# Router logits from the added rows, tile by tile, with two loads re-placed, in a two-layer diffusion block on one core

## The reference

```python
def modulate(h, shift, scale):
    return h * (1 + scale) + shift

def expert_choice_moe(h, w_router, w_gate, w_up, w_down):
    cap = EC_CAPACITY * T // N_EXPERTS
    aff = jax.nn.softmax((h @ w_router).astype(jnp.float32), axis=-1)
    top_w, top_idx = lax.top_k(aff.transpose(0, 2, 1), cap)
    xg = jax.vmap(lambda hb, ib: hb[ib])(h, top_idx)
    ...

# in hybrid_layer
y_l = gated_merge(...)                       # branches -> sum -> @ w_out
x = x + mod_l[2] * y_l
x = x + mod_l[5] * expert_choice_moe(modulate(rms_norm(x, norm2), mod_l[3], mod_l[4]),
                                     moe_router, moe_w_gate, moe_w_up, moe_w_down)
```

## Time and profile before

| | us |
|---|---|
| median of 3 runs | 2647.32 |
| lowest and highest run | 2635.97, 2648.03 |
| profiled execution, its own time | 2637.7 |
| its span in the trace | 2635.9 |
| PE busy | 2479.0 (94%) |
| DVE busy | 1055.8 (40%) |
| ACT busy | 680.8 (26%) |

### The profile page before, as it was taken

One profiled execution on the slowest core, in us unless ns is written; L12 is line 12 of the kernel. 1 busy time (PEld: TensorE's weight loads), 2 busy tenths in 40 slices (PEclk: granted clock), 3 DMA queues, 4 the chain that ended last, 5 costly groups with the idle time before them and its releaser, 6 DMA issues. The chain is left out here.

```text
span 2635.9 us, 41045 instructions
## 1 busy us (share of the span) xinstructions
PE 2479.0 (94%) x17556; PEld 1564.9 (59%) x17556; DVE 1055.8 (40%) x2307; ACT 680.8 (26%) x1348; POOL 87.6 (3%) x145
## 2 busy tenths in 40 slices
PE   5999999999899899999999999999999999999998
PEld 3888877778686444443444588876677643333432
DVE  4545354344774313223231564445348431111113
ACT  3621232222633111111111362143236311010101
POOL 1000100000000000000100000100000000000000
PEclk9999999999999999999999999999999999999999
DMA  6111456151553999897989312322216379999996
GB/s 217 57 49 33 141 197 202 61 168 47 195 175 115 392 346 386 309 396 296 383 331 367 116 41 65 72 94 73 72 57 206 134 288 410 409 409 409 409 409 276
DMA packets 241827, 580.72 MB, mean 220 GB/s; under 512 B 11462, under 2 KB 120240, under 8 KB 240624
## 3 DMA queue, kind: packets, MB, share of 16 engines
q1 hardware_dynamic: 232160, 550.21, 56.0%
q0 software_dynamic: 9488, 27.90, 3.3%
HBM read 554.94 MB, written 23.13 MB: 219 GB/s over the span
## 5 line engine op out<-in xcount | busy, mean ns | idle before, releaser
L1040 PE MATMUL ps<-h_hi,m_lo 128*128 128x512 f32 (+1 forms) x1152 | 347.4, 373 | 2.0 <-DVE arena L2261 1.7
L1481 PE MATMUL ps<-arena 128*32 128x512 f32 x1740 | 259.2, 593 | 1.6 <-ACT arena L1923 1.1
L1482 PE MATMUL ps<-arena 128*32 128x512 f32 x588 | 258.0, 593 | 0.0
L1040 PEld LDWEIGHTS ps<-h_hi,m_lo 128*128 128x128 f32 x1152 | 208.6, 190 | 52.3 <-issue 13.7
L1013 PE MATMUL ps<-m_lo,h_hi 128*128 128x256 f32 (+1 forms) x1248 | 233.7, 289 | 5.2 <-DVE m_lo L2234 2.9
L1040 PE MATMUL ps<-h_lo,m_lo 128*128 128x512 f32 (+1 forms) x576 | 205.5, 357 | 0.0
L1013 PEld LDWEIGHTS ps<-m_lo,h_hi 128*128 128x128 f32 x1248 | 196.6, 195 | 13.7 <-issue 9.7
L1627 PE MATMUL ps<-arena 128*64 128x512 f32 x832 | 187.8, 597 | 11.1 <-DMA arena<-in_moe_w_up 8.5
L1013 PE MATMUL ps<-m_lo,h_lo 128*128 128x256 f32 (+1 forms) x624 | 177.5, 284 | 0.0
L1481 PEld LDWEIGHTS ps<-arena 128*32 128x32 f32 x1740 | 70.3, 110 | 164.2 <-issue 160.7
L1013 PE MATMUL ps<-h_hi,m_lo 128*128 128x512 f32 (+1 forms) x512 | 141.9, 354 | 7.8 <-DVE h_lo L2339 6.9
(11 more groups left out here) (407 smaller groups left out, 4498.8 us busy)
## 6 DMA issues: line engine op xcount, KB each, us to landing
arena<-in_moe_w_up SPq DMA_DIRECT2D x101, 1024.0 KB, 13.0
arena<-in_moe_w_gate SPq DMA_DIRECT2D x100, 1024.0 KB, 11.8
arena<-in_moe_w_down SPq DMA_DIRECT2D x100, 1024.0 KB, 12.8
ring<-in_w_in SPq DMA_DIRECT2D x42, 1024.0 KB, 5.3
arena<-in_ada_w SPq DMA_DIRECT2D x37, 1024.0 KB, 5.6
oT<-in_moe_w_up SPq DMA_DIRECT2D x27, 1024.0 KB, 14.9
oT<-in_moe_w_down SPq DMA_DIRECT2D x24, 1024.0 KB, 9.0
oT<-in_moe_w_gate SPq DMA_DIRECT2D x16, 1024.0 KB, 8.4
```

Source lines behind the costliest of these rows:

```text
L1040: last = mm(to, w[:, k, cols], h[:, k, seg], start=n == 0 and k == 0, stop=n == 2 and k == KD - 1)
L1481: mm(ps[r][32 * b:32 * b + 32, :], c_xg[:, k, j, 32 * b:32 * b + 32], w, start=k == 0, stop=k == KD - 1)
L1482: last = mm(ps[r][96:128, :], c_xg[:, k, j, 32 * r:32 * r + 32], up[:, kk, 512:1024], start=k == 0, stop=k == KD - 1)
```

## The change

1. The router logits are made from the added rows themselves. With r the reciprocal root of a row, g the gain and s the shift, (r x g + s) W = r (x (g W)) + s W. DVE makes `r_gain` = g W and `r_sum`, a partial sum of s W, at the end of `merge` (`router_scaled`, each layer); PE sums the latter over partitions with one product of ones inside the output products, and DVE keeps it (`router_bias`). Per tile PE transposes `x_sb` (8 transposes into two banks), ACT copies one bank and DVE the other, PE makes 8 products with the 128x128 block as stationary operand and 16 moving columns, and DVE applies r and the bias (`logits_kept`). The logits come out with tokens on partitions, so the copy out, the turn back and the four-group sum are gone. Tiles 0 and 1 of the order don't wait for the root.
2. `kept_running(ps[5], 6)` stands behind the logits in both layers. The five fillers ahead of layer 1's transposes are gone.
3. Three late pieces move to the latent attention (7 becomes 10), and all other ten stand behind the transposes of the affinities.
4. The sixth expert load of layer 0 and all behind it wait for `rows_in`, the landing of the first three row fetches. The ninth no longer waits for `lg_up`.
5. Small: `work` is set to -1 behind the softmax's subtraction, two clears of PSUM banks go away, the others clear 260 columns.

```diff
-        ADA = {"first": 8, "na": 20, "mla": 7, "route": 13}
-        UNITS_AHEAD = 2
+        ADA = {"first": 8, "na": 20, "mla": 10, "route": 10}
+        UNITS_AHEAD, LOADS_AHEAD = 2, 5
...
             def route_loads():
-                for h in ada_late("route")[:3]:
-                    late_load(h)
                 sp.wait_ge(y_up, 2 * NQ[0])
-                for h in ada_late("route")[3:10]:
+                for h in ada_late("route")[:7]:
                     late_load(h)
                 sp.wait_ge(y_ok, 2 * NQ[0])
-                late_load(ada_late("route")[10])
-                for h in ada_late("route")[11:]:
+                late_load(ada_late("route")[7])
+                for h in ada_late("route")[8:]:
                     sp.wait_ge(ada_up, h - 7)
                     late_load(h)
...
                     if l == 0 and n == PAIR_SLOTS:
                         sp.wait_ge(xn2_out, 16 * NT)
-                        sp.wait_ge(lg_up, 1)
...
+                    if l == 0 and n == LOADS_AHEAD:
+                        sp.wait_ge(rows_in, 48)
...
+            def router_logits(l):
+                n, y0 = NQ[l], before("y_ok", l)
+                def bank_read(bank):
+                    return y0 + max(q for q in range(2 * n) if 2 + q % 4 == bank) + 1
+                def turned(ti):
+                    t = q_tiles(l)[ti]
+                    first, second = ((ps[6], ps[7]), (ps[1], ps[2]))[ti % 2]
+                    pe.wait_ge(y_ok, max(y0 + n + ti + 1, bank_read(2) if ti % 2 else 0))
+                    if ti >= 2:
+                        pe.wait_ge(h_lat, before("h_lat", l) + ti - 1)
+                        pe.wait_ge(h_ctx, before("h_ctx", l) + ti - 1)
+                    for bank, up, ks in ((first, hl_up, range(4)), (second, hc_up, range(4, KD))):
+                        for k in ks:
+                            last = tr(bank[:, tile(k % 4)], x_sb[:, t, tile(k)], ident)
+                        last.then_inc(up, 1)
+                def logits(ti):
+                    pe.wait_ge(h_lat, before("h_lat", l) + ti + 1)
+                    pe.wait_ge(h_ctx, before("h_ctx", l) + ti + 1)
...
+                    for k in range(KD):
+                        last = mm(ps[(0, 3)[ti % 2]][:, 0:E], xT[ti % 2][:, k, :], r_gain[:, s, k, :], start=k == 0, stop=k == KD - 1)
+                    last.then_inc(lg_up, 1)
+                turned(0)
+                turned(1)
+                for ti in range(n):
+                    logits(ti)
+                    if ti + 2 < n:
+                        turned(ti + 2)
+                kept_running(ps[5], 6)
...
             def route(l):
-                if l == 0:
-                    late_product(ada_late("route")[3])
...
                 last.then_inc(affT_up, 1)
                 if l == 0:
-                    for h in ada_late("route")[5:]:
-                        late_product(h)
-                        late_turned(h - 1)
-                    late_turned(ada_late("route")[-1])
+                    late_products(ada_late("route"))
                     kept_running(ps[5], 3)
...
+            def normed_and_routed(l):
+                s, n = 2 * l + 1, NQ[l]
+                turned_copied(l, 0)
+                scaled(s, n - 2)
+                turned_copied(l, 1)
+                mean(s, n - 1)
+                logits_kept(l, 0)
+                turned_copied(l, 2)
+                scaled(s, n - 1)
+                for ti in range(1, n):
+                    logits_kept(l, ti)
+                    if ti + 2 < n:
+                        turned_copied(l, ti + 2)
...
                 v.tensor_tensor(aff[:, q0:NT, :], lg, st[:, 48 + q0:48 + NT].unsqueeze(2).to_broadcast([P, nt, E]), ALU.subtract
                                 ).then_inc(aff_sh, 1)
+                if NSEG[l] > 1:
+                    link(v.memset(work[0:48, :], -1.0))
```

More of the change, by code:

```diff
@@ L374, in ada_zeroed @@
         def ada_zeroed(h):
-            return 1 + sum(h >= ada_first(stage) for stage in list(ADA)[1:])
+            return 1 + sum(h >= ada_first(stage) for stage in list(ADA)[1:3])
         def late_sums(h):
@@ L1077, in kept_running @@
                     mm(bank[:, :], ident, cst[:, 0:512], start=True, stop=True)
-            def norm_transposes(l):
-                s = 2 * l + 1
-                if l == 0:
[L1083 to L1093, removed]
-                        for k in ks:
[L1095 to L1102, removed]
-                        pe.wait_ge(h_lat, before("h_lat", l) + k - 1)
-                    for t in range(CT, NT):
-                        last = tr(ps[2 + k % 2][:, tile(t - CT)], xn2[:, t, tile(k)], ident)
-                    last.then_inc(hl_up, 1)
-                    if CTX_NORMS[s]:
-                        if k >= 2:
-                            pe.wait_ge(h_ctx, before("h_ctx", l) + k - 1)
-                        for t in range(CT):
-                            last = tr(ps[4 + k % 2][:, tile(t)], xn2[:, t, tile(k)], ident)
-                        last.then_inc(hc_up, 1)
-                    if k == 5:
-                        logits(range(4))
-                logits(range(4, KD)).then_inc(lg_up, 1)
@@ L1401, in merge @@
                         for n, k in enumerate(range(KD) if half else OUT_K):
+                            if (q, n) == (1, 4):
+                                pe.wait_ge(lgT_ok, before("lgT_ok", l) + 1)
+                                mm(ps[6][:, 0:NSEG[l] * E], ones, r_sum[:, 0:NSEG[l], :].rearrange("p a b -> p (a b)"), start=True, stop=True
+                                   ).then_inc(lg_up, 1)
                             for row in gate_rows_beside(l, q, n):
@@ L1811, in scattered_rows_squared, with turned_copied @@
                 rooted(s, NORMS[s] - 1)
-            def modulate(l):
-                s = 2 * l + 1
-                for k in range(KD):
-                    act.wait_ge(hl_up, KD * s + k + 1)
-                    do(hT[:, k, LAT], ps[2 + k % 2][:, :], ACT.Identity, scale=scl[:, 1, k, 0:1],
-                       bias=modT[l][:, 24 + k, 0:1]).then_inc(h_lat, 1)
+            def turned_copied(l, ti):
+                if ti >= 2:
+                    act.wait_ge(lg_up, before("lg_up", l) + ti)
+                act.wait_ge(hl_up, before("hl_up", l) + KD + ti + 1)
+                do(xT[ti % 2][:, 0:4, :].rearrange("p a b -> p (a b)"), ps[(6, 1)[ti % 2]][:, :], ACT.Copy).then_inc(h_lat, 1)
             def modulated_high(l):
@@ L2307, in cleared @@
                 for bank in banks:
[L2308 removed]
+                    last = v.memset(bank[:, 0:260], 0.0)
                 last.then_inc(ada_zero, 1)
@@ L2320, in gains, with router_scaled @@
                                               ALU.add, ALU.mult)
-            def modulate(l):
-                s = 2 * l + 1
-                if CTX_NORMS[s]:
-                    for k in range(KD):
-                        dve.wait_ge(hc_up, KD * sum(CTX_NORMS[:s]) + k + 1)
-                        if k == 0:
-                            v.memset(work[0:48, :], -1.0)
-                        v.tensor_scalar(hT[:, k, CX], ps[4 + k % 2][:, 0:CTX], scl[:, 1, k, 1:2], modT[l][:, 24 + k, 1:2],
-                                        ALU.mult, ALU.add).then_inc(h_ctx, 1)
+            def router_scaled(l):
+                dve.wait_ge(small_in, before("small_in", l) + 48)
+                for s in range(NSEG[l]):
+                    v.tensor_tensor(r_gain[:, s, :, :], router[:, 0:KD, :], scl[:, 1, :, s].unsqueeze(2).to_broadcast([P, KD, E]), ALU.mult)
+                    last = v.tensor_tensor(r_shift[:, s, :, :], router[:, 0:KD, :], modT[l][:, 24:32, s].unsqueeze(2).to_broadcast([P, KD, E]), ALU.mult)
+                link(last)
+                for s in range(NSEG[l]):
+                    last = v.tensor_reduce(r_sum[:, s, :], r_shift[:, s, :, :].rearrange("p k e -> p e k"), AX_X, ALU.add)
+                last.then_inc(lgT_ok, 1)
```

94 lines of the change are left out of this document (43 added, 51 removed).

## The result

The changed kernel took 2659.9 us (median of 6 runs, 2657.8 to 2665.1), the kernel before 2642.2 beside it (2636.0 to 2648.2): ratio 1.0068, 95% interval 1.0046 to 1.0090. It is slower, by 12 to 24 us. The forecast was 2644 within 2633 to 2656, with 0.88 for no change: wrong. The kernel before has three of its runs at 2636 to 2637 and three at 2647 to 2648, and its profile is one of the lower; the changed kernel's runs lie in one place. The changed kernel's profiled execution took 2658.8, its span 2657.0 against 2635.9, so 21.1 us have to be found.

A forecast was written before the change was run, and what follows sets the result against it. PE, busy 94% of the span, was taken to bound the kernel, with loads in layer 1's experts; +3.8 + 0.5 - 2.2 - 0.8 - 0.7 = +0.6 us on 2637.7 gave 2638.3, stated as 2644 for two run places, range 2633 to 2656.

The forecast's parts named there:

- The logits, layer 0: Layer 0's router logits: 14.8 us on PE at 0.116 us a record, then six fillers of 5.3; +0.5 us net.
- Layer 1: Layer 1's routing: logits 9.2 us, then six fillers to 2110.0; affinities' transposes 0.7 us earlier, the experts shifting likewise.
- TensorE's clock falls in the logits: Rival, both layers' logits: 1.2 GHz over their second half and three fillers each, +17 us, 2655; chance 0.06.
- The pieces and the bias: Three late pieces paid in layer 0's latent attention, +3.8 us; bias product in the output products, 0.23 us per layer.
- The fillers eat the gain: Behind layer 0's logits: softmax ready by 854.2, but six fillers delay the affinities' transposes to 856.8, against 856.29 before.
- The fetches: Layer 0's row fetches with five loads ahead: rows at 890.6 against 892.87, -2.2 us, between -3.8 and +2.1.
- The gather behind it: Layer 0's transposes of fetched rows, 6.28 us before: faster after a shorter PE wait, -0.8 us, between 0 and -2.
- Fewer loads ahead: Start of layer 0's experts: loaded weights stay more than one pair ahead, so PE shouldn't wait: 0 us.
- The runs in two places: Whole-kernel times lie at 2636 to 2638 or 2647 to 2648; the new median could fall on either, so 2644.
- The range: Whole-kernel time: 2633 (overlap at the lower place) to 2656 (the clock's case in part, or +8 at the upper place).
- the overlap: Rival, both layers' logits: small products overlap at 0.066 us a record, -7.4 us in all, 2631 to 2637; chance 0.08.

The follow-up runs named there:

- e1: The changed kernel with each logits product reading its router columns eight times over (128 moving columns instead of 16); 2641.8 us, ratio 0.9985.
- e9: The kernel before, with layer 1's five fillers ahead of the transposes replaced by twenty products of 16 columns; 2650.8 us, ratio 1.0019.
- e8: The kernel before with only the load holding added: five expert loads ahead of the rows' first fetch, the others behind; 2635.3 us, ratio 0.9988.
- e4: The changed kernel with layer 0's expert loads no longer held back behind the row fetches; 2665.3 us, ratio 1.0080.
- e3: The changed kernel with 128 moving columns in the logits products and two fillers instead of six; 2634.9 us, ratio 0.9964.
- e2: The changed kernel without the six fillers behind the logits; 2655.7 us, ratio 1.0042.
- e7: The changed kernel with 128 moving columns, two fillers and two expert loads instead of five ahead of the row fetches; 2630.8 us, ratio 0.9963.
- e10: The changed kernel with 128 moving columns, no fillers and two expert loads ahead of the row fetches; 2632.4 us, ratio 0.9957.

## Why the prediction was wrong

The step that failed is the price of the logits in **The logits, layer 0** and **Layer 1**: "per tile 16 records at 0.116, 1.86 us", taken for every tile, and "six take 5.3" for the fillers. 0.116 us is the time of such a record at 2.4 GHz, and it was right for the first tile (1.93 us). I took it to hold for six tiles in a row. The clock fell to 1.2 GHz during the second, and from then on a tile's products took 3.43 and eight transposes 1.95 instead of 1.07.

| stretch, us | predicted | after | e1, 128 columns |
|---|---|---|---|
| layer 0: last output record to the first logits | 3.6 | 3.6 | 3.6 |
| logits of six tiles | 14.8 | 23.8 | 14.3 |
| six fillers | 5.3 | 6.9 | 5.2 |
| affinities' transposes to slot turn | 19.8 | 19.2 | 19.2 |
| slot turn to the fetched rows | 14.0 | 16.6 | 17.5 |
| rows to the experts | 5.5 | 6.4 | 6.5 |
| layer 1: logits of four tiles | 9.2 | 14.2 | 9.0 |
| six fillers | 5.3 | 8.1 | 5.2 |

The four clocked stretches are 18.4 us longer than predicted, and e1 is shorter than the change by 19.5 in them. The rival *TensorE's clock falls in the logits* had this: its place, its point of decision (below 0.8 over 842 to 857; it was 0.54) and nearly its price, 18.4 us for +17, held. The price was partly luck: the rival took half of the logits and half of the fillers, and the clock fell earlier and came back earlier, 14.0 of the 18.4 us being logits and 4.4 fillers. It had a chance of 0.06. What I set against it was that the one stretch at 0.50 that I had seen behind few-column products had also lain behind 2.65 us without work. e9 shows the other half: there the wait ahead is 1.51 us in both kernels, and only with few-column products does the clock fall.

**The pieces and the bias** in latent attention and the output products: last output record at 836.28 against 833.10, 3.2 us for 3.8 + 0.2 predicted. Right, somewhat less. A microsecond of it is scatter: the same record stands at 831.90 in e8, whose program is that of the kernel before up to there, and at 836.04 to 837.41 in the changed kernel's variants.

**The fillers eat the gain**: the mechanism was right and its size was not. Predicted was that the softmax is ready 2.6 us before them; at the full clock (e1) it was 2.8 us in layer 0 and 3.2 in layer 1, and at the fallen one (the changed kernel) 4.6 and 6.2.

**The fetches**: right in sign, mis-sized. The prediction took 5.9 us from third fetch to the rows; it was 8.5, against 10.3 before. Held loads were worth 1.8 us from the slot turn (e4 as well), not 4.3. What was mis-sized is the bytes in the way: five loads, three fetches and 2 us of stores are 7.6 MB from the first load's issue to the rows, and the trace has 8.6 (883.97 to 906.50). The DMA engines were full until 904 and nearly idle behind, the held loads being issued from 906.50 on, so the rows were there some 2 us after the engines had slackened:

```profile
901.00:904.00 3.00, 2.92 (x7) 1.07 (x5) 0.00 (x0) 0.00 (x0) 0.00 (x0) 0.95 1.03 412
904.00:907.00 3.00, 0.52 (x5) 0.52 (x6) 0.00 (x0) 0.00 (x0) 0.00 (x0) 1.00 0.21 85
```

The rows don't wait for all of the queued bytes, though. The third fetch landed 10.2 us after its issue in the kernel before and in e4, with no load held, and also in e3, with five loads ahead; 8.5 in the change; 5.2 to 5.5 in e2, e7 and e8. What differs is how much of the loads is still moved beside the fetches. The view of the DMA queues (packets, MB, share of the engines' time; `q1` carries SP's loads and stores, `q0` POOL's fetches), the kernel before over 880 to 892.87:

```profile
q1 hardware_dynamic: 960, 3.71, 72.0%
q0 software_dynamic: 432, 1.57, 30.6%
```

So `q1` moved 3.7 MB between the first fetch's issue and the rows, and as much in e4; in e3 it was 2.9, in the change 2.3, in e2 0.9, and in e7 0.00 over 882 to 889.2. In the kernel before, nine loads of 1.05 MB had been issued when the first fetch was (the tenth followed at 882.59, the eleventh, at 887.23, behind all three fetches, which the prediction counted otherwise); from the first load's issue to the rows `q1` moved 8.4 MB, less than the nine loads alone. The fetches overtook the rest. The rule of the Trainium skill that the prediction weighed (DMA: Bandwidth & Descriptors, "Queues, rings and completion order"), that an engine takes packets in turn from each queue that has work, agrees with this in kind. The half of the rate that the prediction made of it doesn't: beside the loads the fetches got 30% of the bytes (1.57 of 5.28 MB).

**The gather behind it**, -0.8 predicted: 6.38 us against 6.28, nothing. PE still came out of a wait of 2.56 us where 1.6 was predicted, and the clock was 0.72 over 907 to 913. The gain is real where the wait is short: 5.6 us behind a wait of 0.91 (e7) or none (e2, e8, e10), 6.3 to 6.5 behind 2.20 (e1), 2.56 and 5.93 (e3).

**Fewer loads ahead**: 0 predicted, and no wait for weights in the first turn, neither with five nor, in e7, with two.

**The runs in two places**: the prediction left these unexplained. e8's profile is one of its upper place, with the late pieces at 0.50 throughout. Counted from the last output product its slot turn comes 12.0 us later than in the kernel before (53.4 against 41.4) and its experts start 8.4 us later (74.5 against 66.1), since PE no longer waits for the rows then; e8's two places are 8.4 us apart. That it is the same in the kernel before is likely but not shown, since only an execution of the lower place was profiled. The changed kernel comes to its pieces out of fillers, and its runs lie in one place.

**The range**: its lower end, 2633, is not the prediction's own, since the overlap it stands for was priced at 2631 and less. Nothing hangs on it here.

What stays open: up to 6 us that differ from execution to execution between the experts' start and layer 1's logits (1197.3 us in the changed kernel, 1202.0 in e1, 1200.0 in e3 and e7, 1196.0 in e10). That the ratio doesn't set e7 apart from e3 is in part the two places: it is taken against all runs of the kernel before, of which 17 of 29 lay in the upper place (2650.6 on average) beside e3 and 11 of 23 (2646.5) beside e7. Against the lower place alone e3 is 2.7 us shorter and e7 5.3 (2630.8 against 2636.1).

## What to carry to other kernels

Ask of every new stretch on PE not only how long a record takes but at which clock, and for how long in a row: a rate read from 2.3 us of such records doesn't hold for 15. Where the weight load sets a product's time, more moving columns are nearly free, and here they kept the clock: with eightfold columns the ratio went from 1.0068 to 0.9985. Fillers belong where PE would wait, in the length of that wait; ahead of the only work that the path waits for they are paid in full. Holding back loads helps a fetch by as much as is then no longer moved beside it, so count the bytes still in the queue at the fetch's issue, stores included.

## What the hardware showed that was not expected

A PE without a gap lost its clock. In layer 0 PE and its weight loads were busy for all of the time from 845 to 863 at a granted clock of 0.50, the products having 128x128 stationary operands and 16 moving columns. The Trainium skill (TensorE: Matmul & The Clock Gate, "What's actually happening") ties the clock to how busy PE has been. By the profile's busy time this case doesn't agree; what PE did in it decided. (The ends of PE's records are modelled, so this busy time is not the array's own.) The same page says of transposes that they don't count as PE's being busy in the same way ("Part 4: PE-mode transpose"). Here eight transposes stood between each two tiles in e1 as in the change, and with 128-column products beside them the clock was 1.00; no run here had transposes alone for long. In e9 the clock fell over 16-column products with no transposes among them.

Weight loads of 128 columns hide 128 moving columns almost completely: at the full clock the first tile's 16 records took 1.93 us with 16 moving columns, 1.94 with 32, 1.97 with 64 and 2.02 with 128, and those of a later tile 1.87 with 32, 1.90 with 64 and 1.95 with 128.

The clock can stay low for long under steady work: in e8 PE went through eight late pieces, some 22 us, at 0.50, where the kernel before was back at 1.00 with the second piece.
